# Three transformer layers on one core: heads alternate and rounding comes late in the first attention; GpSimd adds all squares of five norms, and one product with ones spreads their mean

## The reference, cut to what matters

```python
h = rmsnorm(x, norm1_g[i]) * (1.0 + sc1) + sh1
y = sliding_window_sink_attention(h, ...) or stick_breaking_attention(h, ...) or the mixer of layer 3
x = x + g1 * y
h = rmsnorm(x, norm2_g[i]) * (1.0 + sc2) + sh2
x = x + g2 * swiglu(h, w_gate[i], w_up[i], w_down[i])

def rmsnorm(x, gain):
    return x * lax.rsqrt(jnp.mean(x * x, axis=-1, keepdims=True) + EPS) * gain
```

## Time and profile before

| | |
|---|---|
| median of 3 runs | 1057.9 us (1056.94 to 1061.06) |
| profiled execution | 1057.87 us, its span 1056.1 us, mean granted clock 0.948 |
| TensorE, VectorE, ScalarE, GpSimd busy | 994.9, 810.0, 520.9, 31.1 us |
| first attention's steps | about 101 to 159 us |
| the five late norms' sums on TensorE begin | 188.5, 383.4, 527.0, 721.9, 853.2 us |

### The profile page before, as it was taken

How to read it: one execution, slowest core, us unless ns; L and a number is a source line. 1 busy time by engine, 2 the same in 40 slices (tenths; PEclk the granted TensorE clock), 3 DMA queues, 4 the chain that set the end, 5 groups by cost and what they waited for, 6 DMA issues and landing times.

```text
span 1056.1 us, 19739 instructions
## 1 busy us (share of the span) xinstructions
PE 994.9 (94%) x7559; PEld 941.8 (89%) x7559; DVE 810.0 (77%) x1183; ACT 520.9 (49%) x823; POOL 31.1 (3%) x48
## 2 busy tenths in 40 slices
PE   2699879999999999999999999999898899999997
PEld 2587559999999998977999999999788899999997
DVE  6885785899859999675599976999784599986532
ACT  3343763545432376534555442437766574543433
POOL 4000000000000000000000000003000000000000
PEclk9597768999999999999999999999999899999998
DMA  8971349299929979363149992998601528996500
GB/s 299 377 278 43 120 147 332 78 321 329 311 97 380 369 276 319 110 228 131 41 142 307 307 352 101 373 364 269 236 1 51 190 80 298 324 308 233 195 36 40
DMA packets 144416, 232.19 MB, mean 220 GB/s; under 512 B 6250, under 2 KB 75410, under 8 KB 144354
## 3 DMA queue, kind: packets, MB, share of 16 engines
q1 hardware_dynamic: 142993, 228.75, 62.6%
q0 software_dynamic: 1072, 2.05, 0.9%
q10 hardware_dynamic: 288, 0.54, 0.1%
HBM read 230.27 MB, written 1.05 MB: 219 GB/s over the span
## 4 chain that ended last, share of the span: by engine, by line
PE 77%; DVE 11%; ACT 4%; issue 4%; DMA 2%; SPq 1%; DVEq 0%; ACTq 0%
PE M L1575 17%; PE M L1577 17%; PE M L1576 17%; DVE ACC L991 5%; PE AUX L2102 3%; DVE WL L968 2%; PE AUX L1729 2%; DMA RAW<-in_ada_w 1%; ACT WH L596 1%; PE M L1593 1%; PE M L1599 1%; PE M L1595 1%; PE AUX L1642 1%; DMA RAW<-in_wqkv_a 1%; PE M L1647 1%
## 5 line engine op out<-in xcount | busy, mean ns | idle before, releaser
L596 ACT ACTIVATE WH<-RAW 128x2048 fp32r<-128x2048 f32 x136 | 259.3, 1914 | 233.0 <-PE M L1577 74.5
L1575 PE MATMUL M<-XH,WH 128*128 128x256 f32 x1264 | 362.7, 287 | 4.3 <-DVE XL L1065 2.3
L968 DVE TENSOR_TENSOR WL<-RAW,WH 128x2048 fp32r<-128x2048 f32 x136 | 309.4, 2284 | 65.2 <-ACT WH L596 64.8
L1576 PE MATMUL M<-XL,WH 128*128 128x256 f32 x1264 | 358.7, 284 | 0.0
L1577 PE MATMUL M<-XH,WL 128*128 128x256 f32 x1264 | 358.6, 284 | 0.0
L1575 PEld LDWEIGHTS M<-XH,WH 128*128 128x128 f32 x1264 | 243.6, 193 | 6.7 <-issue 4.6
L1576 PEld LDWEIGHTS M<-XL,WH 128*128 128x128 f32 x1264 | 243.7, 193 | 0.2
L1577 PEld LDWEIGHTS M<-XH,WL 128*128 128x128 f32 x1264 | 243.6, 193 | 0.0
L991 DVE SCALAR_TENSOR_TENSOR ACC<-ADA,COND,ACC 128x512 f32<-128x512 f32 x266 | 199.8, 751 | 9.2 <-DMA ADA<-in_ada_w 0.3
L1575 PE MATMUL M<-MH,WH 128*128 (+1 forms) x528 | 149.0, 282 | 2.3 <-DVE WL L968 2.3
L1576 PE MATMUL M<-ML,WH 128*128 (+1 forms) x528 | 148.0, 280 | 0.0
(11 more groups left out here) (279 smaller groups left out, 1370.5 us busy)
## 6 DMA issues: line engine op xcount, KB each, us to landing
ADA<-in_ada_w SPq DMA_DIRECT2D x68, 1024.0 KB, 5.8
RAW<-in_w_gate SPq DMA_DIRECT2D x44, 512.0 KB, 6.3
RAW<-in_w_up SPq DMA_DIRECT2D x44, 512.0 KB, 7.3
RAW<-in_w_down SPq DMA_DIRECT2D x44, 512.0 KB, 7.5
RAW<-in_w_ffn_in SPq DMA_DIRECT2D x44, 512.0 KB, 6.8
RAW<-in_wqkv_b SPq DMA_DIRECT2D x24, 512.0 KB, 5.5
RAW<-in_w_ffn_out SPq DMA_DIRECT2D x22, 512.0 KB, 4.7
RAW<-in_w_in SPq DMA_DIRECT2D x16, 512.0 KB, 8.3
```

The costliest lines, as they stand in the source:

```text
L596: act.activation(WH[:, s, :], RAW[:, s, :], ACT.Copy).then_inc(h_ready, 1)
L968: dve.tensor_tensor(WL[:, s, :], RAW[:, s, :], WH[:, s, :], ALU.subtract).then_inc(l_ready, 1)
L1575: pe.matmul(out_ap, wh, xh, start=start, stop=False, skip_group_check=True)
L1576: pe.matmul(out_ap, wh, xl, start=False, stop=False, skip_group_check=True)
```

## The change

Late norms (n = 1 to 5): GpSimd adds all eight squares into `SQS`. After weight row 3 (not 1) TensorE waits for the seventh addition and forms one product of the 128x128 matrix of 1/1024 with `SQS`, which leaves the mean in every partition of `AUX[:, 0]`; the sums over single tiles and the spread of the root fall away. ScalarE takes the root of 128x256 back into `SQS`, VectorE its reciprocal into `RB`. GpSimd waits for the `RB` of the norm before instead of its sum. VectorE does `low(base, 2)` before the reciprocal instead of between the halves of the scaling. In the feed-forward layers the first half of the `ada_sum` moves from before the first scaled results to behind `low(base, 0, 1)`. Norms 0 and 6 keep three additions.

First attention: the score products of the two heads alternate, with the masks last; so do the output products, which now wait for both heads' weight copies. `high` of `wo_a` units 1 to 3 comes behind the last step, and `low` of these units behind the last step too, with `ada_bias(9)` and `ada_sum(10)` between them.

```diff
--- before.py
+++ after.py
@@ -378,6 +378,14 @@
 IN_COLS = [3 * DA, 2 * DA, DA, 0]
+def sums_added(n, j):
+
+    return sum(3 if m in (0, 6) else KT - 1 for m in range(n)) + j
+
+def spread_at(n):
+
+    return 1 if n == 0 else 2
+
 def unscaled(n, j):
     return (KT + 1) * (n - 1) + j + 2
@@ -558,13 +566,15 @@
     def square_sum(n):
-        if n >= 1:
-            pool.wait_ge(ssq_ready, n)
+        if n == 1:
+            pool.wait_ge(ssq_ready, 1)
+        if n >= 2:
+            pool.wait_ge(rb_ready, n - 1)
         pool.wait_ge(sq_ready, KT * n + 2)
         pool.tensor_tensor(SQS[:, :], TMP[:, 0, :], TMP[:, 1, :], ALU.add).then_inc(sq_sum, 1)
-        for j in range(2, 4):
+        for j in range(2, 4 if n in (0, 6) else KT):
             pool.wait_ge(sq_ready, KT * n + j + 1)
-            pool.wait_ge(sq_sum, 3 * n + j - 1)
+            pool.wait_ge(sq_sum, sums_added(n, j - 1))
             pool.tensor_tensor(SQS[:, :], SQS[:, :], TMP[:, j, :], ALU.add).then_inc(sq_sum, 1)
     for n in range(5):
@@ -618,12 +628,12 @@
         if base is not None:
...
         act.wait_ge(ssq_ready, n + 1)
-        act.activation(STD[:, :], AUX[:, 0, 0:2], ACT.Sqrt, bias=cc(C_EPS)).then_inc(std_ready, 1)
+        if base is not None:
+            act.activation(SQS[:, :], AUX[:, 0, :], ACT.Sqrt, bias=cc(C_EPS)).then_inc(std_ready, 1)
+        else:
+            act.activation(STD[:, :], AUX[:, 0, 0:2], ACT.Sqrt, bias=cc(C_EPS)).then_inc(std_ready, 1)
         if before is not None:
             before()
-        if base is not None:
-            act.wait_ge(rstd_spread, n + 1)
-            act.activation(RB[:, :], AUX[:, 1, :], ACT.Copy).then_inc(rb_ready, 1)
         for j in range(KT):
...
             shift = mod(n // 2, 3 * (n % 2), j)
@@ -792,8 +802,8 @@
             sa_exp(b + 2)
...
         act.activation(XH[:, b, :], AUX[:, 4, :], ACT.Copy).then_inc(hh_ready, 1)
-        if b in (1, 3, 5):
-            high(U0["wo_a"], (b + 1) // 2)
+    for k in range(1, 4):
+        high(U0["wo_a"], k)
     feed_forward(0)
@@ -1075,7 +1085,7 @@
         coefficients(n)
...
         dve.wait_ge(coef_ready, n + 1)
-        dve.wait_ge(rstd_spread, n + 1)
+        dve.wait_ge(rstd_spread, spread_at(n))
         for j in range(KT + 2):
...
                 scaled(n, j, AUX[:, 1, :])
@@ -1086,7 +1096,11 @@
         fill = 3 * (n // 2) + 2 * (n % 2)
         low(base, 1)
-        root(n)
+        low(base, 2)
+        if n >= 2:
+            dve.wait_ge(first_scaled, 4 * (n - 1))
+        dve.wait_ge(std_ready, n + 1)
+        dve.reciprocal(RB[:, :], SQS[:, :]).then_inc(rb_ready, 1)
         dve.wait_ge(rb_ready, n)
...
             for j in range(4 * half, 4 * half + 6):
@@ -1094,7 +1108,8 @@
                     scaled(n, j, RB[:, :])
...
                     scaled_low(n, fill, j - 2)
-            low(base, 2 + half)
+            if half == 1:
+                low(base, 3)
     def feed_forward(layer, before):
@@ -1122,7 +1137,6 @@
         low(base, 0)
...
         late_norm(2 * layer + 1, base)
-        ada_sum(b0, int(b0 >= 24), rows=range(0, 4))
         td = BD[f"gu{layer}"]
...
         dve.tensor_copy(BI[:, 0:2], FIRST_BIAS[0]).then_inc(bi_ready, 1)
@@ -1134,6 +1148,7 @@
         for n in range(2):
...
         low(base, 0, 1)
+        ada_sum(b0, int(b0 >= 24), rows=range(0, 4))
         dve.wait_ge(bi_ready, 4 * layer + 2)
...
             dve.wait_ge(silu_ready, m0 + n + 1)
@@ -1372,10 +1387,11 @@
         half = KT // 2 * (b % 2)
...
         attn_low(1, b)
-        if b in (1, 3, 5):
-            low(U0["wo_a"], (b + 1) // 2)
+    low(U0["wo_a"], 1)
     ada_bias(9)
+    low(U0["wo_a"], 2)
     ada_sum(10, 0)
+    low(U0["wo_a"], 3)
     add_out("wo_a", 0, 0)
     def before_ffn_a():
@@ -1649,10 +1665,9 @@
                     mm.then_inc(bank_done, 1)
...
                 mm.then_inc(w_used, 1)
-            if kt == 1:
-                norm_sums(n)
-            if kt == 2:
-                norm_spread(n)
+            if kt == 3:
+                pe.wait_ge(sq_sum, sums_added(n, KT - 1))
+                pe.matmul(AUX[:, 0, :], ONES, SQS[:, :], start=True, stop=True).then_inc(ssq_ready, 1)
     def values(base, k, kts, col, width, outs, first, last):
@@ -1704,14 +1719,14 @@
         for j in range(4, 6):
             mean_square(n, j)
-        pe.wait_ge(sq_sum, 3 * n + 3)
+        pe.wait_ge(sq_sum, sums_added(n, 3))
         token_means(AUX[:, 0, 0:2], SQS, ONES[:, 0:1], False, False)
...
     def norm_spread(n):
-        pe.wait_ge(rstd_ready, n + 1)
+        pe.wait_ge(rstd_ready, spread_at(n))
         spread(AUX[:, 1, :], RSTD, 0).then_inc(rstd_spread, 1)
     def norm(n, blocks=()):
@@ -1883,12 +1898,16 @@
     def sa_scores(b):
+        pair = []
         for e in range(2):
...
             keys = QA[rows, 8, :] if e == b // 4 else KS[rows, :]
-            bank = MB[:, 2 - 2 * (b % 2) + e, :]
+            pair.append((MB[:, 2 - 2 * (b % 2) + e, :], rows, keys))
+        for bank, rows, keys in pair:
             pe.matmul(bank[:, 0:P], QA[rows, b, 0:P], keys[:, 0:P], start=True, stop=False, skip_group_check=True)
+        for bank, rows, keys in pair:
             pe.matmul(bank[:, P:3 * P], QA[rows, b, P:2 * P], keys, start=False, stop=False, skip_group_check=True)
+        for bank, rows, keys in pair:
             mm = pe.matmul(bank[:, 0:3 * P], IDB[:, :], MASKA[:, :], start=False, stop=True, skip_group_check=True)
         mm.then_inc(sa_s, 1)
@@ -1906,13 +1925,15 @@
         kv = slice(HD * (b // 4), HD * (b // 4) + HD)
...
             pe.wait_ge(xin_ready, KT + b)
+        pe.wait_ge(sa_ptc, 2 * b + 2)
+        outs = [AUX[HD * e:HD * e + HD, 4, :] for e in range(2)]
         for e in range(2):
-            pe.wait_ge(sa_ptc, 2 * b + e + 1)
-            rows = slice(HD * e, HD * e + HD)
-            o = AUX[rows, 4, :]
-            pe.matmul(o[:, 0:P], VA[:, 0, kv], PT[:, b % 2, e, 0:P], start=True, stop=True, skip_group_check=True)
-            pe.matmul(o[:, P:2 * P], VA[:, 0, kv], PT[:, b % 2, e, P:2 * P], start=True, stop=False, skip_group_check=True)
-            mm = pe.matmul(o[:, P:2 * P], VA[:, 1, kv], PT[:, b % 2, e, 2 * P:3 * P], start=False, stop=True, skip_group_check=True)
+            pe.matmul(outs[e][:, 0:P], VA[:, 0, kv], PT[:, b % 2, e, 0:P], start=True, stop=True, skip_group_check=True)
+        for e in range(2):
+            pe.matmul(outs[e][:, P:2 * P], VA[:, 0, kv], PT[:, b % 2, e, P:2 * P], start=True, stop=False, skip_group_check=True)
+        for e in range(2):
+            mm = pe.matmul(outs[e][:, P:2 * P], VA[:, 1, kv], PT[:, b % 2, e, 2 * P:3 * P], start=False, stop=True,
+                           skip_group_check=True)
         mm.then_inc(sa_o, 1)
```

## The result

The changed kernel takes 1067.8 us (median of 9 runs, 1058.47 to 1070.09) against 1062.0 for the kernel before (9 runs beside it, 1056.94 to 1063.71): ratio 1.0053, 95% interval 1.0029 to 1.0077. It is slower by half a per cent, 5.8 us. The profiled execution took 1061.61 us with a span of 1059.8, 3.7 longer than the one of before. The forecast was 1066.9.

The account below looks back on a forecast made before the run. TensorE was taken as the bound, in the attention the handing over between engines. From 1057.87 us, -10.0 + 23.1 - 1.65 + 6.6 - 9.0 = +9.05 gave 1066.9 us; range 1039 to 1072.

Parts of the forecast that it names:

- Late norms on TensorE: Late norms 1 to 5: one product replaces the tiny sums and the root's spread, saving 2.0 us each, 10.0 us.
- What GpSimd must do: Late norms: open additions wait behind two rounding rests, so TensorE waits 4 x 5.3 + 1.9 = +23.1 us.
- the second rival: Late norms: additions and VectorE instructions take turns at every boundary, norms cost 14.5 us, total 1055.0 us; chance 0.22.
- Clock: Late norms: TensorE runs at its lower clock level after four waits of 5 us, 4 x 1.65 = +6.6 us.
- The credit of 1.65: Norm 4: the clock drop behind the tiny products goes away with them, -1.65 us.
- Attention: First block's attention: roundings leave the loop and score products overlap, saving 9 us (6 to 13) over three pairs.
- my bound of 4.2 from the high clock: Attention: at most 4.2 us saved per pair of heads at the high clock, VectorE needing at least 10.7 a pair.
- The bound from the low clock: Attention: TensorE at 1.2 GHz needs 16.9 us a pair, 13 with overlapped score products, so 1.9 saved per pair.
- Late roundings under the projection: Three weight roundings behind the last head are covered by the output projection: nothing; without the cover up to 4 us.
- The root: Late norms: wide root and reciprocal cost nothing, covered by four weight rows (5.8 us) before TensorE needs the scaled rows.
- my bound of 1.5: Late norms: the 256-column reciprocal on VectorE takes 0.47 to 1.5 us, taken as 1.2.
- The moved sums: Feed-forward: moved conditioning sums start queued SP transfers some 2.4 us later, against several microseconds of slack: nothing.

Follow-up runs that it names:

- moved_loads_first: Kernel before with feed-forward conditioning sums moved behind the first scaled results and next rest, conditioning-weight load behind all four weight loads: 1058.8 us, ratio 0.9992.
- attention_alone: Kernel before with only the attention's part of the change (alternated heads, late weight roundings), norms and conditioning sums as before: 1047.0 us, ratio 0.9886.
- attention_loads_first: Kernel before with the attention's part of the change, and the conditioning-weight load on SP behind all four weight loads of a step: 1044.5 us, ratio 0.9860.
- late_roundings_alone: Kernel before with only the three weight roundings of the output projection moved behind the last head: 1048.4 us, ratio 0.9897.
- alternation_alone: Kernel before with only the alternation of the two heads' score and output products: 1053.4 us, ratio 0.9934.
- sums_moved_alone: Kernel before with only the four feed-forward conditioning sums moved behind the first scaled results and the next rest: 1068.4 us, ratio 1.0088.
- changed_loads_first: Changed kernel with the conditioning-weight load on SP behind all four weight loads of a step instead of behind the second: 1057.4 us, ratio 0.9971.

## Why the prediction was right in its number and wrong in its terms

**The time.** The forecast was 1066.9 us, and 1067.8 were measured, but that closeness is luck in two ways. The forecast stood 9.05 us above the profiled execution of the kernel before, 1057.87; the runs beside the changed kernel had a median of 1062.0, and the change cost 5.8. And the 9.05 has the right sign and size only because three terms, off by 4.8, 11.9 and 16.6 us, cancelled. The main effects were found: the attention gains, and the additions make TensorE wait.

**Late norms on TensorE: right.** The forecast saved 2.0 us per norm; group 1, which has no wait, is 1.9 shorter. The new product took 0.66 us with its restart (174.12 to 174.78), forecast 0.5.

**What GpSimd must do: the step that failed.** From "Of four boundaries between VectorE instructions without a gap it won one" I let the open additions come in only behind low(1) and low(2), 5.3 us of waiting in each of norms 2 to 5. But at a rest an addition gets in every time. The waits for the sum were 0, 4.8, 2.2, 4.8 and 0 us, 11.7 in all and not 23.1; in norm 5 there were 1.5 for the first rest. What I had as the second rival, turns, gave -10 + 14.5 + 3.3 - 1.65 = +6.15 for the norms, and the first groups measured +6.1; its single norms were off by up to 1.7 us. The Trainium skill (SBUF — State Buffer, "Who interferes with whom") states the rule behind that rival: a VectorE instruction with two SBUF inputs and a GpSimd instruction that reads SBUF lock each other out, and the order of issue decides who blocks. The 2.83 and 2.58 us above agree with it, the additions of 1.43 and 1.83 us among short instructions do not. I had set the rival aside for four boundaries between instructions of 0.47 us and applied their ratio to instructions of 2.28.

**Clock: right in kind.** The two waits of 4.8 us brought the lower level and cost 2.2 and 1.6 us (group 4: 18.9 - 14.4 + 1.9 - 4.8), the wait of 2.2 us cost nothing: 3.8, not 6.6. The credit of 1.65 for the dip in norm 4 named the wrong place. In seven traces with the old norm a dip of 1.5 us stands in six, in one first group each: group 4 before and in moved_loads_first, group 1 in attention_alone (15.92 us) and attention_loads_first, group 2 in late_roundings_alone (15.93), group 3 in alternation_alone (15.95), none in sums_moved_alone. In the six traces with the new norm groups 1, 3 and 5 are free of it. So the credit may well be due, but it isn't norm 4's, and no run isolates its cause.

**Attention: right mechanism, term too small.** It gave 13.8 instead of 9. A pair saved 4.8 us, above my bound of 4.2 from the high clock. That bound was VectorE's floor of 10.7, which is 0.6 too high: its four terms add up to 5.30 and not 5.35, one step in two begins its conditioning sum with the cheaper form, 0.48 instead of 0.75 us, and other starts lie closer than the durations. The bound from the low clock has a slip too: with 1.58 us less in each of its two steps the 16.9 become 13.7 and not 13, so it should have been 1.2 saved and not 1.9. Between the two I took a middle, on the ground that a TensorE that waits for VectorE loses the high level. In the changed kernel it was busy only 7.2 of 10.1 us of such a pair and was granted 1.00.

**Late roundings under the projection: right, nothing.** From the projection's start to the first norm's group it is 25.5 us before and 24.5 in attention_alone.

**The root: wrong.** The prediction says: "So this part costs nothing with either price". The reciprocal took 1.74 us, above my bound of 1.5, and in the three feed-forward norms the cover I named did not exist. I had checked it against TensorE's need of the scaled rows, not against what VectorE has to do behind them. Norm 2 had the cover: the stretch behind group 2 is 129.2 in both kernels.

**The moved sums: wrong.** The prediction has the transfers start "some 2.4 us later, against roundings with several microseconds of slack there". They started 3.7 to 4.6 us later, and there was no slack: ScalarE already waited 3.35 us for one of them in the kernel before. That row was in the trace and I had not looked for it. The price was 7.4 us.

**Open.** Of the first feed-forward stretch's 5.4 us, 1 us is in no wait of TensorE that I can name. Why the additions of norms 2 and 4 are passed over among the short instructions and those of norm 5 are not was not tried.

## What to carry to other kernels

Before you price a moved instruction at nothing, follow what its semaphore releases: if that stands at the head of an in-order queue, everything behind it moves too, and the engine to ask is the one that already waits for those transfers. Time saved on the engine with the largest share is kept only where the next engine has slack in the same stretch; compare both from a common mark (here VectorE's 25.6 and 26.5 us from the start of the first group) and not by their shares of the span. And a number that comes out right over terms of both signs proves none of them: time each part alone.

## What the runs showed of the hardware

A VectorE reciprocal of 128x256 in f32 took 1.74 us where a pass over that shape takes 0.47 (128x16 took 0.24).

The same seven additions have more than one course. In group 4 of the changed kernel six of them took 10.61 us; in group 4 of changed_loads_first, with the same instructions on both engines, they took 5.67, and the group 14.4 us instead of 18.9. Norm 5 of the changed kernel itself has the short course. First the two norms of the changed kernel, then the other.

```profile
716.16 10.61 POOL L578 TENSOR_TENSOR SQS<-SQS,TMP 128x256 f32<-128x256 f32 x6
...
849.15 5.45 POOL L578 TENSOR_TENSOR SQS<-SQS,TMP 128x256 f32<-128x256 f32 x6
```

```profile
717.40 5.67 POOL L578 TENSOR_TENSOR SQS<-SQS,TMP 128x256 f32<-128x256 f32 x6
...
719.36 3.11 DVE L1064 SCALAR_TENSOR_TENSOR UL<-X,COEF,UH 128x256 fp32r<-128x256 f32 x4
```

In changed_loads_first the additions get in between the short UL instructions as well (0.78 us each instead of 0.54 in group 4 of the changed kernel), and are done before the second rest begins. So a wait of 4.8 us hangs on how two engines' instructions happen to lie, which a forecast from one trace can't settle.
